# Expert lists of a mixture layer: all lists in one written order, with a closing loop and rows picked by matrix product

## What is computed

```python
logits = (xf @ w_router)
top_vals, top_idx = lax.top_k(logits, 2)
gates = softmax(top_vals)
# for each of the 8 experts e, over the rows routed to it:
y = (silu(x @ w1[e]) * (x @ w3[e])) @ w2[e]      # 1024 -> 3584 -> 1024
out[token] += gate * y
```

## Time and profile before

| | |
|---|---|
| median of 3 runs | 1874.23 us |
| profiled execution, its own time | 1873.73 us |
| its span, first to last instruction | 1871.8 us |
| TensorE busy | 1800.9 us (96%) |
| VectorE, ScalarE busy | 989.1 us (53%), 778.4 us (42%) |
| DMA over the span | 532.99 MB, mean 285 GB/s |

### The profile page before, as it was taken

The page is one execution under the profiler, slowest core; times in us unless marked ns, Lnnn a source line. Parts: engine busy times, 40 slices in busy tenths (PEclk is TensorE's granted clock), DMA queues, the critical chain, the costliest instruction groups (busy, mean ns, idle before and its releaser), DMA issues.

```text
span 1871.8 us, 28142 instructions
## 1 busy us (share of the span) xinstructions
PE 1800.9 (96%) x11305; PEld 1359.7 (73%) x11305; DVE 989.1 (53%) x1143; ACT 778.4 (42%) x997; POOL 161.4 (9%) x139
## 2 busy tenths in 40 slices
PE   9999999999999999999999999999999999999976
PEld 8977898777988999988877788755555555555532
DVE  6877643467766655577779898821212222221102
ACT  7766533445354543435557677611211222121100
POOL 0032020000011400010203100000000000000000
PEclk9999999999999999999999999999999999999999
DMA  6533477514753655566169999999999999999996
GB/s 249 192 113 105 169 281 268 180 48 161 265 178 126 241 182 193 188 223 208 46 239 350 408 388 365 370 364 393 423 424 423 424 423 416 415 423 423 424 424 258
DMA packets 81096, 532.99 MB, mean 285 GB/s; under 512 B 9472, under 2 KB 12800, under 8 KB 20432
## 3 DMA queue, kind: packets, MB, share of 16 engines
q1 hardware_dynamic: 72704, 501.60, 68.7%
q0 software_dynamic: 7664, 28.64, 4.4%
q10 hardware_dynamic: 608, 1.07, 0.2%
HBM read 513.30 MB, written 14.42 MB: 282 GB/s over the span
## 4 chain that ended last, share of the span: by engine, by line
PE 80%; DVE 7%; DMA 7%; ACT 3%; issue 2%; POOL 0%; DVEq 0%; SPq 0%; ACTq 0%
PE bank L800 72%; DMA ring<-in_w_moe 6%; DVE whi L3272 2%; ACT whi L2387 2%; DVE wrest L3024 1%; PE bank L1015 1%; PE bank L1382 1%; DVE wrest L2430 0%; DMA cst<-in_consts 0%; PE bank L1681 0%; PE bank L1018 0%; PE bank L1189 0%; PE bank L1103 0%; PE bank L1133 0%; PE bank L1389 0%
## 5 line engine op out<-in xcount | busy, mean ns | idle before, releaser
L800 PE MATMUL bank<-ring,arena 128*64 128x256 f32 (+1 forms) x2032 | 243.7, 390 | 9.9 <-DMA ring<-in_w_moe 9.9
L800 PEld LDWEIGHTS bank<-ring,arena 128*64 128x64 f32 x2032 | 142.2, 137 | 107.6 <-issue 34.9
L3024 DVE TENSOR_TENSOR wrest<-ring,whi 128x2048 fp32r<-128x2048 f32 x88 | 203.8, 2357 | 20.7 <-ACT whi L2261 18.9
L800 PE MATMUL bank<-hTh,wrest 128*128 128x256 f32 x608 | 171.3, 282 | 0.0
L2261 ACT ACTIVATE whi<-ring 128x2048 fp32r<-128x2048 f32 x84 | 157.1, 1917 | 22.1 <-DMA ring<-in_w_moe 21.0
L3272 DVE TENSOR_TENSOR whi<-ring,whi 128x2048 fp32r<-128x2048 f32 x31 | 71.1, 2292 | 178.2 <-ACT whi L2387 178.2
L3221 DVE TENSOR_TENSOR arena<-arena,bank 128x256 f32<-128x256 f32 x35 | 14.7, 420 | 211.0 <-ACT arena L2333 211.0
L2430 DVE TENSOR_TENSOR wrest<-ring,fhi 128x2048 fp32r<-128x2048 f32 x33 | 76.5, 2317 | 81.9 <-ACT fhi L1838 81.8
L800 PEld LDWEIGHTS bank<-hTh,wrest 128*128 128x128 f32 x608 | 114.9, 189 | 0.0
L800 PE MATMUL bank<-arena 128*64 128x256 f32 (+2 forms) x832 | 104.8, 372 | 3.7 <-DMA arena<-in_w_moe 3.0
L800 PE MATMUL bank<-ring,bvr 128*64 128x512 f32 x432 | 102.6, 598 | 4.6 <-DMA ring<-in_w_moe 4.4
(11 more groups left out here) (550 smaller groups left out, 4125.6 us busy)
## 6 DMA issues: line engine op xcount, KB each, us to landing
ring<-in_w_moe SPq DMA_DIRECT2D x274, 1024.0 KB, 9.5
ring<-in_w_dense SPq DMA_DIRECT2D x135, 1024.0 KB, 5.0
arena<-in_w_moe SPq DMA_DIRECT2D x62, 1024.0 KB, 10.4
row<-in_rows POOLq DMA_DIRECT2D x17, 512.0 KB, 5.5
xg_rows<-ncR POOLq DMA_DIRECT2D x10, 512.0 KB, 22.4
arena<-arena SPq DMA_DIRECT2D x32, 106.5 KB, 4.2
arena<-in_tbias POOLq DMA_DIRECT2D x2, 1536.0 KB, 8.9
y_rows<-ncR POOLq DMA_DIRECT2D x5, 512.0 KB, 40.2
```

The costliest lines, as they stand in the source:

```text
L800: ins = pe.matmul(out_, lhsT, rhs, start=start, stop=stop, **more)
L3024: S["w_lo"].on(v.tensor_tensor(wrest[:, s, :], ring[:, s, :], whi[:, n % HI_SLOTS, :].bitcast(F32), ALU.subtract))
```

## The change

- The loop over 128-row lists is gone. Ranks 1, 2 and 0 (`HEAVY_RANKS`) stand in one written order with the four lists of ranks 3 to 6: 294 pieces. A heavy step now runs its six pieces in turn with small ones between: in a mid step one after piece 1, two after piece 3 and one after piece 5, and in a wide step 17 of them. The step's own product is turned one small piece after its piece 3 (two in wide steps).
- The list of rank 7 and any overflow run in a closing loop of 64-row lists, 1 to 5 trips. Here it is one trip of 42 small pieces, which follows from the profile before: SP issued 336 pieces there, which is 8 experts with no extra list, so no list is over its room.
- The ring has 9 buffers in the written order and 7 in the loop; pieces are split three places ahead (`LOOK`). The first four pieces are all mid pieces, so nothing is multiplied twice.
- xg_rows, its zeroing, the scatter and the loads are gone. TensorE picks the rows of each further list from h by 16 fp32 matmuls (`gather_list`), four times in the written order (after pieces 3, 20, 30 and 60) and once in each trip; VectorE makes the 0/1 matrices (`choose`).
- Waits in the written order are held against constants.

```diff
-    big = [("big", d, c) for d in range(E_STEPS) for c in range(6)]
-    places = {k if k < 2 else 6 + (k - 2) * 21 // 4 for k in range(len(big))}
-    small, big = iter(small), iter(big)
-    return [next(big) if m in places else next(small) for m in range((1 + N_SMALL) * E_CHUNKS)]
+    heavy = []
+    for u in range(HEAVY_STEPS):
+        heavy += [(u, c) for c in range(6)]
+    after_mid, after_big = (0, 1, 0, 2, 0, 1), (3, 2, 3, 4, 2, 3)
+    order, small, wanted = [], iter(small), 0
+    for u, c in heavy:
+        order.append(("heavy", u, c))
+        if u == 0 and c < 3:
+            continue
+        some = after_mid[c] if u < MID_STEPS else after_big[c] - (u == HEAVY_STEPS - 1 and c != 3)
+        for _ in range(some):
+            order.extend([s] if (s := next(small, None)) else [])
+    return order + list(small)
...
-LATE_RING, LATE_HI = 8, 4
+LATE_RING, LATE_HI, LOOP_RING, LOOK = 9, 4, 7, 3
...
-                b = m + 2
-                if b in SPLIT_NO and b >= AHEAD:
+                b = m + LOOK
+                if b in HEAVY_NO and b >= AHEAD:
...
+            def gather_list(width):
+
+                for k in range(KT):
+                    bank, at_ = (6 + k // 4, k % 4 * P) if width == P else (6, k * HALF)
+                    for j in range(2):
+                        ins = pe.matmul(ps[bank][:, at_:at_ + width], h[:, j, k * P:(k + 1) * P], sel[:, j, 0:width],
+                                        start=j == 0, stop=j == 1, skip_group_check=True)
+                S["p_g"].on(ins)
...
+            trips = pe.value_load(plan_i[0:1, ID_TRIPS:ID_TRIPS + 1], min_val=1, max_val=MAX_TRIPS)
+            wait(pe, "b_hT64", E_STEPS)
+            with pe.Fori(0, trips) as t:
+                wait(pe, "x_sel", t + (len(GATHERS) + 1))
+                gather_list(HALF)
```

More of the change, by code:

```diff
@@ L140 @@
 TURN_AT = [AT["small", t, 3] + 1 for t in range(SMALL_STEPS)]
[L141 to L145, removed]
+HEAVY_TURN_AT = [AT["heavy", u, 3] + (1 if u < MID_STEPS else 2) for u in range(HEAVY_STEPS)]
+GATHERS = ((ROW_64, P), (ROW_SMALL + HALF, P), (ROW_SMALL + 3 * HALF, HALF), (2 * P, P))
@@ new lines, with stored_by @@
+HI_SLOT = _hi_slots()
+Y_DONE = sorted([(AT["heavy", E_STEPS * e + E_STEPS - 1, 5], "heavy", e) for e in range(3)]
+                + [(AT["small", E_STEPS * l + E_STEPS - 1, 5], "small", l) for l in range(N_SMALL - 1)])
+Y_PARTS = [2 if kind == "small" else 3 if n == 2 else 1 for _, kind, n in Y_DONE]
+Y_STORES = sum(Y_PARTS)
+def stored_by(kind, n):
+    k = [part[1:] for part in Y_DONE].index((kind, n))
+    return ZEROED + 16 * sum(Y_PARTS[:k + 1])
+LOOP_ORDER = [part for j in range(E_STEPS) for part in [(j, c) for c in range(4)] + ([(j - 1, 4), (j - 1, 5)] if j else [])]
@@ L149, in in_expert @@
+LOOP_ORDER += [(E_STEPS - 1, 4), (E_STEPS - 1, 5)]
+LOOP_AT = {part: n for n, part in enumerate(LOOP_ORDER)}
 def in_expert(j, c):
@@ L550, in _ @@
                         stack(i)
[L552 to L563, removed]
@@ L1750, in big_second, with turn_heavy @@
+                if d >= 0:
+                    if half == 0:
+                        wait(pe, "b_hT64", d + 1)
+                    w = late_raw(m).rearrange("p (k n) -> p k n", k=2)
+                    for k in range(2):
+                        ins = whole_halves(ps[7][:, :], hT_64[:, k, half_columns(half, HALF)], w[:, k, :], 512,
+                                           first and k == 0, last and k == 1)
                 chunks_used.on(ins)
-            def turn_big(d):
-                wait(pe, "b_hid", d + 1)
+            def turn_heavy(u):
+                wait(pe, "b_hid", u + 1)
@@ new lines, in _ @@
+            wait(a, "router_done", 2)
+            trips = a.value_load(plan_i[0:1, ID_TRIPS:ID_TRIPS + 1], min_val=1, max_val=MAX_TRIPS)
+            with a.Fori(0, trips) as t:
+                wait(a, "p_g", t + (len(GATHERS) + 1))
+                S["p_xa"].on(a.activation(loop_x, ps[6][:, :].rearrange("p (k n) -> p k n", k=KT), ACT.Copy))
+                for j in range(E_STEPS):
+                    step = t * E_STEPS + (SMALL_STEPS + j)
+                    a.wait_ge(chunks_used.sem, t * E_CHUNKS + (N_DENSE + STATIC + LOOP_AT[j, 3] + 1))
+                    silu_small(step)
+                    copy_small(step, hT_small[j % 2])
@@ L3268, in _ @@
+                if m == AT["heavy", E_STEPS - 1, 3] + 1:
+                    rest_gathered(1, 6)
+                for e in range(2):
+                    if m == AT["heavy", E_STEPS * e + E_STEPS - 1, 5] + 1:
+                        keep_mid(e)
+                if m == AT["heavy", HEAVY_STEPS - 1, 5] + 1:
                     keep_big()
-                b = m + 2
-                if b in SPLIT_NO and b >= AHEAD:
-                    wait(v, "w_hi", mids * E_CHUNKS + (MOE_ROUNDED + SPLIT_NO[b] + 1))
+                b = m + LOOK
@@ L3286, in _ @@
+            wait(v, "ple_done", 20)
+            v.wait_ge(tb_in, trips * 64 + 32)
+            for q in range(4):
+                if q >= 2:
+                    v.wait_ge(S["m_fe"].sem, q - 1)
+                S["m_fe"].on(v.scalar_tensor_tensor(fe[:, q % 2, :], yg[q], weight[:, q:q + 1], fe[:, q % 2, :],
+                                                    ALU.mult, ALU.add))
             v.wait_ge(S["m_fe"].sem, 4)
```

847 lines of the change are left out of this document (385 added, 462 removed).

## The result

The change took 1883.58 us (median of seven executions, 1880.04 to 1885.58), the kernel before 1875.49 beside it (seven, 1873.33 to 1876.70): a ratio of 1.0042 with a 95% interval of 1.0032 to 1.0052, thus **slower by 0.42%, 8 us**. The profiled execution took 1883.58, its span is 1881.8.

The account below looks back on a forecast made before the run. TensorE was taken to bound the whole written order by a little, DMA the closing loop. Terms of -0.9 up to piece 294 and -0.1 for the last 42 made -1.0 against 1873.73: 1872.7 us, range 1857 to 1887.

Parts of the forecast that it names:

- rival B: Heavy steps: split and turn collide on VectorE, holding TensorE 0.93 in each of 21, 19.5 us, so 1892; chance 0.22.
- Term 7: New waits of TensorE in the written order: first step 3.8, 2 for 20 other heavy steps; +5.8 us, bounds 3 and 25.
- the sum: Terms up to the end of piece 294: -0.9 us, so it ends at about 1749.6.
- The last 42 pieces: Closing loop, from the end of piece 294: 104.5 us where it was 104.6, -0.1; bounds 3 less, 5 more.
- The load of the number of trips: Entry into the closing loop, on VectorE: between 0 and 1.3 us, taken at 1.3.
- terms 1 and 3: Up to piece 294: double products of four pieces gone, -6.9 us; turns of loaded rows gone, -3.8 us.
- term 2: TensorE's old waits gone: 6.0 in the loop, 1.9 behind it, 13.9 + 3.5 in the written order; -25.3 us.
- picks of 128 and 64 columns: TensorE's row picks in the written order: three of 128 at 3.65 each, one of 64 at 3.5; +14.5 us.
- A wide step: Written order: TensorE needs 60.0 us for 23 pieces, DMA 56.9.
- Term 5: Mid steps: 42 changes of form between plain and split matmuls at 0.28 each, +11.8 us; bounds nothing and 15.

Follow-up runs that it names:

- experiment 1: The change, with ScalarE rounding the heavy piece three places ahead before, not after, copying a small step's turned product in mid steps: 1874.64 us, ratio 1.0005.
- experiment 5: The change with rounding ahead of the small copy and mid steps' small pieces in two groups of two: 1875.96 us.
- experiment 8: The change with rounding first, two groups of small pieces, last list's picks early with y copy behind the loop's first gate, second 0/1 matrix later: 1869.27 us, ratio 0.9966.
- experiment 11: All edits of experiment 8 except the rounding first: 1869.49 us, ratio 0.9963.
- experiment 10: Experiment 7 plus eight useless fp32 matmuls ahead of the picks at the closing loop: 1873.79 us.
- experiment 4: The change with the small pieces of mid steps in two groups, not three: 1874.63 us, ratio 0.9996.
- experiment 7: Experiment 1 with VectorE's second 0/1 matrix moved behind the rest of the first heavy step's product: 1875.19 us, ratio 0.9987.

## Why the prediction was wrong, step by step

The forecast was no change, 1872.7; it was slower by 8 us. What happened is the mechanism of rival B, at under half its price (8.6 us went with the edit of experiment 1, where B had 19.5), with a loss of clock on top that the text didn't have.

- **Term 7 failed.** I priced the first step at 3.8 and "2 for the 20" others. The first step took less, 1.2 and 1.5; the others took 7.9: 2.8 in the second, 3.5 in the pattern, and one of 1.6 in the seventh, which stayed when the order was mended. That is 10.6 for 5.8. What I had written, that rests are issued early because the raw data is there, left out that the rounding ahead of the rest can be held: on ScalarE it stands behind a copy that waits for a turn of TensorE. I had looked at what stands on VectorE at the turn and not at what ScalarE's queue waits for two pieces earlier. Nor did it have the operation of POOL that lengthens a rest. With the order mended (experiment 1), the waits are 4.4, and piece 294 ends 787.9 after the first mid piece starts, where the sum had 787.8.
- **Rival B** had this, but once in each of 21 heavy steps and at 0.93. It came in 5 of the 14 mid steps: four times at 0.8 to 0.9 (0.5 to 0.6 before the turn and 0.3 behind it), once at 0.5 and 2.3, and never in a wide step.
- **No term had the clock.** The change lost 1.7 us behind the wait at 1011 and another 1.7 in 960 to 965 (granted 0.66; so did experiment 1, but not 5, 8 and 11, nor the kernel before), and the picks at the loop took 5.21 and not 3.5 (3.79 in experiment 1, at full clock).
- **The last 42 pieces** were 110.0 for 104.5. The windows of the change and of experiment 1 here:

```profile
1740.00:1760.00 20.00, 18.68 (x92) 9.67 (x89) 5.53 (x10) 2.18 (x2) 1.65 (x3) 0.99 0.83 319
1760.00:1780.00 20.00, 17.58 (x134) 12.04 (x135) 1.11 (x2) 1.36 (x3) 4.95 (x6) 0.84 0.80 313
```
```profile
1740.00:1760.00 20.00, 17.92 (x126) 11.54 (x124) 3.56 (x9) 0.60 (x1) 2.71 (x5) 1.00 0.82 304
1760.00:1780.00 20.00, 17.48 (x138) 9.66 (x134) 0.84 (x2) 1.53 (x4) 3.89 (x4) 1.00 0.99 405
```

  Against 423 GB/s DMA missed 10.1 us of work in the change ((104 + 110) x 20 / 423), where the forecast had 5 of standing still. At full clock, in experiment 1, it missed 6.5 and the stretch took 107.7. So about 2.3 of the 5.5 goes with the clock, by these two profiles, and 1.5 with a longer stand of DMA. Its slightly lower rate behind (421) makes 0.4; the last 1.3 stays open. The load of the number of trips, taken at 1.3, cost nothing that shows: the 0/1 matrix was ready 1.4 us behind piece 294, where I had 2.8. The fixed cost that the prediction takes from the Trainium skill (DMA: Bandwidth & Descriptors, Anatomy of one DMA) is stated there for DMAs that GpSimd issues, while SP issues these pieces; no run here separates such a cost.
- **Right:** TensorE bound the written order (180.00 of 180 us busy), the double products and the turns went (terms 1 and 3) and so did the old waits (term 2) but for one, and picks of 128 and 64 columns cost the same: in the written order the 64-column ones took 3.68 and the others 3.73, so the row of 8-column matmuls was the better guide. A wide step was 60.06 to 60.72 for 60.0.
- **Wrong, but offset.** The wait that stayed is the 1.73 ahead of the first mid piece: it is in the 6.0 of term 2 and is still there, 1.82 (959.66 above), so term 2 took off 1.7 too much. Term 5 was too low: 0.36 to 0.4 for a group and not 0.28, 3.4 to 5 us over 42 of them; with these two, the 1.7 us of clock and waits of 4.4 for 5.8, the sum for experiment 1 would be 5 to 7 us above the 787.9 measured. What offsets them the runs don't show, so the hit of 787.9 for 787.8 is in part luck.

With the collision out, experiment 1 and the kernel before agree to 0.05%, as the forecast claims: picks and changes of form take back what the mixing saves in waits. Experiment 8 shows that this balance is not fixed: with fewer changes of form and no picks at the loop the mixed order is 0.34% faster.

## What to carry to other kernels

In a static order, look for what each queue waits for, not only what it has to do: one short copy that needs a late result holds every rounding behind it, and the wait shows two engines further on. When TensorE has no slack, every wait of 1 to 3 us is a risk beyond its length, since the clock may fall behind it; single fixes may then gain nothing beside each other and yet add up together, as in experiment 8. Taking away an obstacle (the picks) can bare another wait that it had covered.

## What was not expected of the hardware

- **The granted clock fell behind waits as short as 1.3 us, in experiment 10 behind one of 0.77, but not each time.** Behind 1.32 at the loop it fell in the change and not in experiment 1. Behind a wait of 2.72 us, experiment 5 ran its first picks at half clock for a part and experiment 11 ran them at full (3.84 above):

```profile
973.85 5.47 PE L1575 MATMUL bank<-arena,h 128*128 128x128 f32 x32 [2.72 <-DVE arena L3109]
```

  At 1.2 for 2.4 GHz a fall cost between 1.7 us (1010 to 1020 in the change) and 3.3 on the picks of experiment 4 alone (7.09 for 3.79). Executions of one kernel differ along with it: in experiment 7, 1870 at 0.998 and 1876 at 0.995. What decides whether it falls, the runs don't show.
- **VectorE's rest took 4.29 for 2.29 us beside an operation of POOL of 2.37 us.** The Trainium skill (SBUF — State Buffer, SBUF: two separate sides) says that a VectorE operation with two SBUF inputs and a GpSimd one that reads SBUF exclude each other, the later one standing for the whole of the other. The trace agrees: the rest that started 0.2 us behind POOL's operation took 2.0 longer, and in experiment 1, where the rest came first, POOL's took 0.8 longer. The last operation of the first 0/1 matrix (0.34 us alone, 2.49 when POOL came at the same moment) is a second case, and made 2.5 us between executions of like kernels.
- **Fp32 picks cost by the matmul and not by the column:** 32 recorded matmuls take 3.68 us with 64 columns and 3.73 with 128, and behind a wait 3.79 and 3.84.
